# Two-layer decoder trunk on one core: 16 bytes more in each row block of the normed activations and of the memory tokens

## The reference, cut to what matters

```python
for layer in range(DEPTH):                     # DEPTH = 2
    h = rmsnorm(x, g[0])
    m = mixer_ab(h, ...) if layer % 2 == 0 else mixer_cd(h, ...)
    x = x + rmsnorm(m, g[1])
    h = rmsnorm(x, g[2])
    x = x + rmsnorm(cross_attn(h, mem, xa_wq[layer], xa_wkv[layer], xa_wo[layer]), g[3])
    h = rmsnorm(x, g[4])
    x = x + rmsnorm(sq_relu_mlp(h, mlp_w1[layer], mlp_w2[layer]), g[5])
```

## Time and profile before

| | |
|---|---|
| median of 3 runs | 932.8 us |
| the runs | 932.37, 932.80, 936.82 us |
| span of the profiled execution, first to last instruction | 935.2 us |
| TensorE matmul (PE) busy | 890.5 us, 95% |
| weight load (PEld) busy | 866.8 us, 93% |
| VectorE, ScalarE, GpSimd busy | 68%, 50%, 19% |
| mean granted TensorE clock | 0.990 of full speed |
| moved from HBM | 151.58 MB, 163 GB/s over the span |

### The profile page before, as it was taken

The page is one execution under the profiler, slowest core; times in us unless marked ns, Lnnn a source line. Parts: engine busy times, 40 slices in busy tenths (PEclk is TensorE's granted clock), DMA queues, the critical chain, the costliest instruction groups (busy, mean ns, idle before and its releaser), DMA issues.

```text
span 935.2 us, 17320 instructions
## 1 busy us (share of the span) xinstructions
PE 890.5 (95%) x7354; PEld 866.8 (93%) x7354; DVE 638.7 (68%) x1006; ACT 468.9 (50%) x663; POOL 173.9 (19%) x165
## 2 busy tenths in 40 slices
PE   8899998999999999999989998999998799999996
PEld 7899998998989999999889988899998799999996
DVE  4686996687497555554779999855884675555552
ACT  6664554565465444444543333365653554444443
POOL 1120800000001000000048778655000010000000
PEclk9999999999999999999999999999999899999999
DMA  8454434544555656655645665444632355655551
GB/s 297 130 179 135 136 122 149 181 136 142 166 178 177 198 183 192 190 184 178 199 127 178 196 183 181 136 160 156 194 122 90 115 180 186 191 185 181 185 176 46
DMA packets 82821, 154.92 MB, mean 166 GB/s; under 512 B 6822, under 2 KB 8760, under 8 KB 82744
## 3 DMA queue, kind: packets, MB, share of 16 engines
q1 hardware_dynamic: 82632, 153.77, 52.3%
q10 hardware_dynamic: 112, 0.05, 0.0%
HBM read 151.58 MB, written 1.05 MB: 163 GB/s over the span
## 4 chain that ended last, share of the span: by engine, by line
PE 66%; DVE 21%; ACT 6%; POOL 2%; issue 2%; DMA 2%; DVEq 0%; SPq 0%; POOLq 0%; ACTq 0%
PE ps L556 20%; PE ps L557 20%; PE ps L558 20%; DVE w_lo L1420 8%; ACT w_hi L1036 3%; DVE ps L1765 2%; DMA raw<-in_ab_w_in 2%; POOL w_lo L2050 2%; DVE tmp L1703 1%; DVE h_lo L1431 1%; DVE xc L1487 1%; DVE xT L1710 1%; PE ps L778 1%; DVE cv L1938 1%; PE ps L918 1%
## 5 line engine op out<-in xcount | busy, mean ns | idle before, releaser
L1036 ACT ACTIVATE w_hi<-raw 128x1024 fp32r<-128x1024 f32 x284 | 295.2, 1054 | 231.4 <-DMA raw<-in_mlp_w 130.7
L1420 DVE TENSOR_TENSOR w_lo<-raw,w_hi 128x1024 fp32r<-128x1024 f32 x238 | 290.7, 1244 | 141.0 <-ACT w_hi L1036 137.0
L556 PE MATMUL ps<-h_hi,w_hi 128*128 128x256 f32 x1248 | 353.0, 283 | 20.8 <-DVE w_lo L1420 11.3
L557 PE MATMUL ps<-h_lo,w_hi 128*128 128x256 f32 x1248 | 349.9, 280 | 0.0
L558 PE MATMUL ps<-h_hi,w_lo 128*128 128x256 f32 x1248 | 349.8, 280 | 0.0
L556 PEld LDWEIGHTS ps<-h_hi,w_hi 128*128 128x128 f32 x1248 | 238.5, 191 | 25.2 <-DVE w_lo L1420 12.4
L558 PEld LDWEIGHTS ps<-h_hi,w_lo 128*128 128x128 f32 x1248 | 237.1, 190 | 0.0
L557 PEld LDWEIGHTS ps<-h_lo,w_hi 128*128 128x128 f32 x1248 | 236.8, 190 | 0.1
L556 PE MATMUL ps<-r_hi,w_hi 128*128 128x256 f32 x512 | 144.3, 282 | 0.0
L558 PE MATMUL ps<-r_hi,w_lo 128*128 128x256 f32 x512 | 144.1, 281 | 0.0
L557 PE MATMUL ps<-r_lo,w_hi 128*128 128x256 f32 x512 | 144.1, 281 | 0.0
(11 more groups left out here) (269 smaller groups left out, 1252.4 us busy)
## 6 DMA issues: line engine op xcount, KB each, us to landing
raw<-in_mlp_w SPq DMA_DIRECT2D x128, 512.0 KB, 3.8
raw<-in_cd_w_in SPq DMA_DIRECT2D x40, 512.0 KB, 3.9
raw<-in_xa_wkv SPq DMA_DIRECT2D x32, 512.0 KB, 3.8
raw<-in_ab_w_in SPq DMA_DIRECT2D x24, 512.0 KB, 4.5
raw<-in_xa_wq SPq DMA_DIRECT2D x16, 512.0 KB, 4.0
raw<-in_xa_wo SPq DMA_DIRECT2D x16, 512.0 KB, 3.8
raw<-in_cd_w_out SPq DMA_DIRECT2D x16, 512.0 KB, 3.9
raw<-in_ab_w_out SPq DMA_DIRECT2D x12, 512.0 KB, 3.7
```

What stands on the lines that cost most here:

```text
L556: nc.tensor.matmul(dst, wt[0], x[0], start=start, stop=False, skip_group_check=True)
L557: nc.tensor.matmul(dst, wt[0], x[1], start=False, stop=False, skip_group_check=True)
L1036: nc.scalar.activation(w_hi[:, v % SLOTS, :, :], raw[:, v % SLOTS, :, :], ACT.Copy)\
L1420: V.tensor_tensor(w_lo[:, v % SLOTS, :, :], raw[:, v % SLOTS, :, :], f(w_hi[:, v % SLOTS, :, :]), ALU.subtract).then_inc(lo_ready_dve, 1)
```

## The change

Each of the four tensors gets rows of 260 words instead of 256, and the view leaves out the last four, so a K block starts 1040 bytes behind the one before it instead of 1024. The two skips ahead of the pairs go, and the third is 64 bytes shorter, so that all from `v_hi` on stays where it was. What lies between (`k_hi`, `k_lo` up to `tmp`) moves by 64 bytes.

```diff
         xT = sb("xT", [J, T])
-        skip(256)
-        mem_hi, mem_lo = sb("mem_hi", [J, T], F32R), sb("mem_lo", [J, T], F32R)
-        skip(192)
-        h_hi, h_lo = sb("h_hi", [J, T], F32R), sb("h_lo", [J, T], F32R)
+        mem_hi, mem_lo = (sb(n, [J, T + 4], F32R)[:, :, 0:T] for n in ("mem_hi", "mem_lo"))
+        h_hi, h_lo = (sb(n, [J, T + 4], F32R)[:, :, 0:T] for n in ("h_hi", "h_lo"))
@@
         tmp = sb("tmp", [2, T])
-        skip(352)
+        skip(288)
```

## The result

The changed kernel takes 940.46 us (median of 9 runs) against 932.8 us before: 0.8% slower, ratio 1.0078 with a 95% interval of 1.0061 to 1.0095. (One of the nine, of 1089 us, stood apart from all others and is not in the ratio.) The forecast was 942 us. Its profiled run took 939.75 us with a span of 938.0 us.

A forecast was written before the change was run, and what follows sets the result against it. The prediction took TensorE (PE) as the bound, busy 890.5 of 935.2 us. h +10.4, mem -0.6, scores -0.3 and absorbed waits -0.4 us gave +9.1, rounded to +9: 932.8 + 9 = 942 us; own range 938 to 947, whole range 917 to 951 us.

The forecast's parts named there:

- The signs that the prediction named: In the profile after: h durations towards 282 ns, MLP h blocks 11.33 us, steps varying by K block, mem below 283 ns.
- The step after: h matmuls after the change: 118.3 ns, from lines drawn between distance levels; +10.4 us over 3840 matmuls.
- The step before: h matmuls before the change: 115.6 ns, the middle of two levels, 113.4 and 117.8 ns.
- What is absorbed: Where PE waits for w_lo, mostly in projections, a slower PE waits less: -0.4 us, a sixth of 2.7 us.
- The small terms: Outside h's step: mem moving -0.6 us, scores -0.3 us, writers 0, V no change within +-1 us.
- Nothing happens: Rival: steps differ for another reason, h keeps its two levels; 933 us, chance 0.20.
- The faster case: Rival: staggered blocks keep the streams apart, h and mem matmuls at 113.4 ns or below; 921 us, chance 0.30.
- The worst level: Rival: rows off a multiple of 64 bytes cost more than a bad distance, +16.1 us for h; 949 us, chance 0.04.

The follow-up runs named there:

- experiment 1: Against the changed kernel: only h_hi and h_lo keep the wider rows, mem back where it stood before; 940.44 us, ratio 1.0075.
- experiment 5: Against the kernel before: rows of 1024 bytes, h_hi and h_lo both at constant distance 112 modulo 256; 933.06 us, ratio 0.9989.
- experiment 6: Against the kernel before: rows of 1024 bytes, h_hi and h_lo both at constant distance 0 modulo 256; 946.34 us, ratio 1.0126.
- experiment 4: Kernel without the model's work, groups of 48 matmuls at distances in steps of 16 bytes, three pauses; settled steps 113.3 to 120.0 ns.
- experiment 7: Against the changed kernel: h, mem, r, mh, my, mp, scores' and attention's operands at 112 modulo 256, V at 144; 924.86 us, ratio 0.9893.
- experiment 2: Against the kernel before: rows of 1024 bytes, h_hi at constant distance 256, h_lo at 384; 940.34 us, ratio 1.0076.
- experiment 10: Kernel without the model's work: stationary offsets change per matmul, moving operand's distance kept from next weights, its own, or neither; those steps 117.2 to 118.9 ns.
- experiment 3: Against the kernel before: h_hi and h_lo share rows of 2064 bytes, both at distance 448 + 16 j; 939.15 us, ratio 1.0062.
- experiment 8: Kernel without the model's work: distances in steps of 4 bytes, plus 512 moving columns; nothing below 113.3 ns, 512 columns 226.7 to 236.7 ns.

## Why the prediction was right

**The mechanism, by its own steps.** PE was the bound, and the h matmuls' step set the time: shown by experiments 1 (only h), 5 and 6 (only h's place; 0.9989 against 1.0126). Placement matters at equal type and shape: shown by experiments 4 to 7. The signs that the prediction named came out: h's mean duration rose to 282 ns; the h blocks of both MLPs take 11.32 and 11.31 us for 96 (11.33 forecast) and no longer differ; the step changes with the K block (117.2 ns at 336 to 118.8 ns at 320 for h_hi; 116.0 ns at 448 to 120.3 ns at 464 for h_lo); mem fell below 283 ns; r stayed.

**The step after.** 118.3 ns forecast, 117.9 ns measured. The way to it was weaker than the number, and that the two lie so close is in part luck. I drew straight lines between four distances; the map of experiment 4 shows that there are no such lines (96: 120.0, 112: 113.3, 128: 118.7 ns). The row that I called nearest, my's 118.2 ns, came out of a window; my's 184 steps average 117.3 ns in the same trace. What the runs put in its place: a stretch whose distances are constant falls into one settled rhythm, 113.3 ns at best and 120.0 ns at worst among multiples of 16 bytes; a stretch whose distances change gets neither in the mean. Experiments 1 and 2 have h at 117.9 and 117.7 ns, the stretches of experiment 10 lie at 117.2 to 118.9 ns. The level still depends on the distances: experiment 3 has 117.3 ns, with K blocks from 114.9 to 118.8 ns. The prediction had this in its sentence that a changing distance leaves little time to settle, but priced nothing on it.

**The step before.** I took 115.6 ns from the one profile there was. Three executions give 115.65, 114.90 and 114.43 ns, and the profiled one was the slowest of them. I had noted that it stood above the median and treated the difference as a constant offset. Most of what moves between executions is the very thing that the change acts on: 1.22 ns x 3840 = 4.7 us of the 5.1 us between the first and the third. With their mean, 115.0 ns, the change costs 2.9 ns x 3840 = 11.1 us in steps, where I had 10.4 us.

**What is absorbed: the term most mis-sized.** I let 0.4 us go. All starts of a trace sorted by the gap in front of the next (sums in us, in brackets the number of gaps; 256 columns are the products of three, V and fp32 all the rest):

| gaps | before, 1st | before, 2nd | before, 3rd | after, 1st | after, 2nd |
|---|---|---|---|---|---|
| 256 columns, under 140 ns | 757.3 (6474) | 754.6 (6474) | 755.1 (6492) | 764.4 (6473) | 765.2 (6481) |
| 140 to 260 ns | 24.1 (116) | 24.0 (115) | 20.2 (97) | 25.5 (122) | 23.7 (113) |
| over 260 ns: waits | 36.0 (34) | 36.7 (35) | 36.0 (35) | 29.6 (29) | 30.4 (30) |
| V and fp32 | 109.4 | 109.2 | 110.2 | 110.0 | 111.1 |

The waits are 6.2 us shorter after (36.2 and 30.0 us in the mean; 0.6 us of this is the plain step within the 5 gaps by which they are fewer). About half of that is in one place, layer 1's input projection with its 864 matmuls, where they sum to 9.7, 10.4 and 11.7 us before and 7.2 us in both executions after. Its waits for w_lo in the third execution of before, and in the first of after:

```profile
PE ps L556 <- POOL w_lo L2050: 6.7, 5, 1.9
PE ps L556 <- DVE w_lo L1420: 2.5, 4, 0.8
```

```profile
PE ps L554 <- POOL w_lo L2048: 4.8, 5, 1.7
PE ps L554 <- DVE w_lo L1418: 0.7, 1, 0.7
```

In that stretch the weights' low parts set the pace, not PE, so slower matmuls only shorten the wait. From the first of these 864 matmuls to the first behind them it took 110.4, 110.2 and 110.2 us before, with h's step at 116.8, 115.7 and 114.2 ns, and 110.4 and 110.5 us after, at 117.8 ns. I had named such places and let a sixth of their share go; here it was all of it.

By the table the change costs +9.1 us in steps under 140 ns, +1.8 us in gaps of 140 to 260 ns, -6.2 us in waits and +1.0 us in V and fp32, +5.7 us in all, and the spans say the same (932.7 and 938.5 us in the mean). In the prediction's terms that is +11.1 us for h (10.4 forecast), -1.0 us for mem and scores (-0.9), +0.7 us for V (0) and -6.2 us absorbed (-0.4), +4.6 us together; the last 1.1 us had no term, and matmuls at 1.2 GHz are in it (last section). The ratio says +7.3 us, because the three profiled executions of before took 934.5 us in the mean, 1.7 us more than the median of its nine runs. So the forecast of +9 us had one size right and one far too small, and that it lies 1.5 us from the median of the changed kernel is luck in part: a little more for h and V, what it had no term for, and the runs of before that were faster than its profiled ones made up for most of the absorption that it missed.

**The small terms.** mem: -0.6 us forecast, 1.8 ns x 384 = -0.7 us measured. Scores: -0.3 us forecast; the step of k falls from 118.60 to 115.97 and 115.02 ns, -0.3 us. Writers: 598 to 596 ns and 602 to 594 ns, nothing, as forecast. V: I took no change, and it is 0.7 us slower, inside the bound of 1 us; the map gives 226.7 ns at distance 0, which mem had, and more at every other place.

**The rivals.** "Nothing happens" is out: r, with its distance kept, holds its level and h doesn't. The faster case was out for h as placed, but a kernel of its kind exists (experiment 7), and its size had the right order: 925 us against 921. The worst level was realised by experiment 6, by a constant distance of 0 and not by odd row starts: h at 119.9 ns, 946 us. The Trainium skill, "SBUF — State Buffer", section "Who interferes with whom", by which PE never waits on anyone, would have every place alike; the maps disagree, 113.3 to 130.0 ns for one and the same shape by address alone, though they don't show whether a port is the reason.

**What stays open.** Why one distance is fast. Experiment 10 excludes that the distance to only one of the two stationary operands decides; that both do together, or that a change of address costs by itself, it leaves open. Whether it is a conflict of reads, and between which, no run here shows. Why the attention's product is slow at the distance that is fast elsewhere isn't known, so the slices' own place may count too. What tips a stretch into one of the two rhythms at 192 isn't known either, beyond that a different pause before it can.

## What to carry to other kernels

Where a dense stream of matmuls is the bound, the placement of the moving operand relative to the weight slots is worth a measurement: place all of it at one constant distance, here 112 modulo 256 bytes for 256 columns, rather than stagger it, and read the step of each group afterwards, since one group here was slow at that distance too. The gain was 1.1% with everything placed so, and nothing clear of noise with h alone, which stood well before. Before a small change is sized from a profile, ask whether the term that it acts on is the same in every execution; one profile can't say, and a profiled run above the median is a hint that it isn't. And a slower or faster matmul counts only where PE is the bound: take the stretches in which it waits for its weights out of the count first.

## What the runs showed of the hardware

- The step of a 128x128 matmul with 256 fp32r columns at 2.4 GHz is 113.3 to 130.0 ns by the distance of its operands modulo 256 bytes, and never less, at 64 places (experiments 4 and 8). Several settled levels are whole multiples of 6.67 ns, over one step (113.33 and 120.0 ns) or over three (3 x 117.78 = 353.3 ns); 118.33 ns is not.
- At 64 and 192 two rhythms are open, 113.3 and 117.8 ns. One held through seven h blocks of an MLP, with r blocks of 96 matmuls at 118.7 ns between them. The kernel before ran between 930.3 and 936.8 us by its first 9 runs, the changed one between 938.6 and 941.2 us in the eight of the ratio.
- The granted clock fell from 2.4 to 1.2 GHz at places that partly differ between executions and versions. Stretches (length, PE busy with the matmuls that start, clock, DMA share, GB/s) at 33 us: the first execution of before, which has a fall there as the second has, and the third:

```profile
33.00:36.50 3.50, 3.46 (x17) 0.54 0.27 100
```

```profile
33.00:36.50 3.50, 3.50 (x33) 1.00 0.00 0
```

  17 matmuls start in the first row and 33 in the second, which is worth 16 x 0.11 = 1.8 us. The changed kernel had no such fall there and one at 477 us, right behind the stretch of 470 to 474 us in which PE waited in part:

```profile
470.00:474.00 4.00, 3.28 (x26) 1.00 0.45 134
477.30:481.00 3.70, 3.70 (x21) 0.54 0.00 0
```

  That stretch can't be the whole reason: PE waited longer in it before (2.95 of 4.00 us busy), and no fall followed.
- The length of a fall near 737 us (729 to 742 us by version) goes with h's step. It lasts 6.8 us in the three executions of before and in experiments 5 and 7, and 10.2 us in the six executions with h at 117.3 ns or more (the change twice, experiments 1, 2, 3 and 6). The first execution of before, and of after:

```profile
743.30:746.60 3.30, 3.30 (x31) 1.00 0.38 104
```

```profile
743.30:746.60 3.30, 3.30 (x18) 0.50 0.00 0
```

  In the 3.3 us shown 13 fewer matmuls start, worth some 1.5 us. How the longer steps bring it about, if they do, is not shown, but a time that is worked out from steps alone leaves it out.
